# Sparse attention over paged keys and values: keys and values of a chunk loaded by different queues at different times

## The reference, cut to what matters

```
past = cache_nsa_kv[l][page_table].reshape(bs, past_len, 4, N_KV, N_HD)
...
sq = jnp.einsum('bqghd,bgqsd->bghqs', qb, kg).astype(jnp.float32) * scale + bsel
ps = masked_softmax(sq, (d >= 0)[:, :, None])
return jnp.einsum('bghqs,bgqsd->bqghd', ps.astype(vg.dtype), vg)
```

## Time and profile before

| | |
|---|---|
| median of 3 runs | 2291.73 us (2290.72 to 2292.28) |
| span of the profiled execution | 2293.0 us, its own time; no other time of it is given |
| PE busy | 2180.6 us (95%) |
| PE weight loads | 1997.7 us (87%) |
| DVE, ACT, POOL busy | 1271.6, 844.5, 592.2 us |
| mean granted TensorE clock | 0.971 of full speed |
| page chunk transfers (`na_kv<-in_pool`) | 128 from SP, 128 from POOL, 128 KB each |
| median us to landing | 3.6 (SP), 4.1 (POOL) |

### The profile page before, as it was taken

How to read it: one execution, slowest core, us unless ns; L and a number is a source line. 1 busy time by engine, 2 the same in 40 slices (tenths; PEclk the granted TensorE clock), 3 DMA queues, 4 the chain that set the end, 5 groups by cost and what they waited for, 6 DMA issues and landing times. The chain is left out here.

```text
span 2293.0 us, 42808 instructions
## 1 busy us (share of the span) xinstructions
PE 2180.6 (95%) x17107; PEld 1997.7 (87%) x17107; DVE 1271.6 (55%) x2352; ACT 844.5 (37%) x1712; POOL 592.2 (26%) x508
## 2 busy tenths in 40 slices
PE   9999998989888889999999999999899999999997
PEld 7799977865555569999999988899899999999997
DVE  2213445247666671123237145566899887876957
ACT  4221244216656560011234133553333433334443
POOL 0000025412232211211111300242344433445633
PEclk9999989979999999999999999998999999999998
DMA  4211187973453431111311156232223232265234
GB/s 152 101 44 46 37 143 236 324 279 125 131 166 111 125 128 56 60 42 56 105 63 37 38 213 244 100 131 84 89 94 117 71 122 89 85 234 186 91 119 147
DMA packets 133712, 276.33 MB, mean 121 GB/s; under 512 B 24626, under 2 KB 79571, under 8 KB 128332
## 3 DMA queue, kind: packets, MB, share of 16 engines
q1 hardware_dynamic: 110796, 232.32, 30.5%
q0 software_dynamic: 10368, 28.33, 3.8%
q10 hardware_dynamic: 12352, 12.96, 1.8%
HBM read 229.49 MB, written 48.26 MB: 121 GB/s over the span
## 5 line engine op out<-in xcount | busy, mean ns | idle before, releaser
L88 PE MATMUL psum<-merged_high,oq_half 128*128 128x352 f32 x768 | 189.0, 326 | 1.9 <-POOL oq_half L69 1.4
L88 PE MATMUL psum<-ff_t,ff_x_slots 128*128 128x264 f32 x1200 | 149.1, 284 | 1.3 <-DVE ff_x_slots L69 1.3
L88 PEld LDWEIGHTS psum<-ff_t,ff_x_slots 128*128 128x128 f32 x1200 | 147.1, 188 | 1.6 <-issue 1.5
L88 PEld LDWEIGHTS psum<-merged_high,oq_half 128*128 128x128 f32 x768 | 135.2, 190 | 2.5 <-POOL oq_half L69 1.9
L1655 POOL DMA_DIRECT2D na_kv<-in_pool x128 | 69.0, 539 | 228.0 <-PE psum L1859 157.8
L88 PE MATMUL psum<-x_half_high,mg_w_high 128*128 128x352 f32 x384 | 124.0, 323 | 2.1 <-ACT gated L2340 1.2
L88 PE MATMUL psum<-h_again_low,mg_w_high 128*128 128x352 f32 x384 | 123.1, 321 | 0.0
L88 PE MATMUL psum<-x_half_high,mg_w_low 128*128 128x352 f32 x384 | 123.0, 320 | 0.0
L1957 ACT ACTIVATE na_pt<-psum 128x512 f32<-128x512 f32 (+1 forms) x170 | 86.5, 543 | 89.3 <-PE psum L1832 80.8
L88 PE MATMUL psum<-ff_bslot,ff_x_slots 128*128 128x264 f32 x888 | 117.8, 286 | 0.7 <-DVE ff_z L4305 0.7
L88 PEld LDWEIGHTS psum<-ff_bslot,ff_x_slots 128*128 128x128 f32 x888 | 112.5, 189 | 1.0 <-DVE ff_z L4305 0.9
(11 more groups left out here) (668 smaller groups left out, 5607.0 us busy)
## 6 DMA issues: line engine op xcount, KB each, us to landing
na_kv<-in_pool SPq DMA_DIRECT2D x128, 128.0 KB, 3.6
na_kv<-in_pool POOLq DMA_DIRECT2D x128, 128.0 KB, 4.1
ff_bslot_raw<-mid_ops SPq DMA_DIRECT2D x59, 264.0 KB, 3.1
mid_ops<-ff_bufs SPq DMA_DIRECT2D x11, 1056.0 KB
mg_w<-in_w_merge SPq DMA_DIRECT2D x15, 768.0 KB, 4.5
ring<-in_f_wu SPq DMA_DIRECT2D x11, 1024.0 KB, 5.3
low<-in_f_wg SPq DMA_DIRECT2D x22, 512.0 KB, 4.5
first_pages<-in_pool SPq DMA_DIRECT2D x68, 128.0 KB, 5.7
```

What stands on the lines that cost most here:

```text
L88: ins = nc.tensor.matmul(out, w[a], x[b], start=first and n == 0, stop=last and n == 2)
```

## The change

SP loads the keys of all 16 pages of a chunk, and waits for the scores of chunk m-2 only (`scores_ready`). POOL loads the values of all 16 pages, and waits for the values of chunk m-2 (`pv_ready`), as before. Each page gives two transfers of 128 rows x 512 bytes (64 KB) in place of one of 128 KB: SP and POOL issue 16 a chunk each where they issued 8. The page numbers are read in two halves: those of sequences 0 and 1 before the slot wait, those of 2 and 3 between the eighth and the ninth transfer. PE waits for the keys at the scores and for the values at the values product. The window chunks are laid out like the page chunks and are loaded by SP as 4 transfers of keys and 4 of values, with a semaphore each. The slot wait of the chunks 0 and 1 is unchanged.

```diff
-        kv_loaded = [sem(f"kv_loaded{j}") for j in range(2)]
+        keys_loaded = [sem(f"keys_loaded{j}") for j in range(2)]
+        window_values = [sem(f"window_values{j}") for j in range(2)]
...
-        SP_PAGES, POOL_PAGES = [(b, p) for b in (0, 1) for p in range(4)], [(b, p) for b in (2, 3) for p in range(4)]
...
-        def slot_free(eng, m):
-
-            if m >= 2:
+        def slot_free(eng, m, part):
+
+            if m == 0:
+                eng.wait_ge(S["hm_kept"], 16)
+            elif m == 1:
+                eng.wait_ge(S["scores_ready"], logits_done(at[OWN_BIAS, 0, 0]))
+            elif part == KEY:
+                eng.wait_ge(S["scores_ready"], logits_done(chunk_items[m - 2]))
+            else:
                 eng.wait_ge(S["pv_ready"], order[chunk_items[m - 2]] + 1)
...
-        def load(eng, m, mine, done):
+        def load(eng, m, part, done):
             _, s, c = chunk(m)
-            page = [g for b in range(mine[0][0], mine[-1][0] + 1)
-                    for g in page_numbers(nc, eng, pages, (4 * s + b) * NPAGE + 4 * c, 4, N["n_pool"])]
-            slot_free(eng, m)
-            for (b, p), g in zip(mine, page):
-                eng.dma_start(kv[m % 2][:, b, 2 * PAGE * p:2 * PAGE * (p + 1)],
-                              A["pool"][ds(g, 1), :, 2 * PAGE:4 * PAGE].rearrange("a p x -> (a p) x")).then_inc(done[m % 2], 16)
+            for half in range(2):
+                page = [page_numbers(nc, eng, pages, (4 * s + b) * NPAGE + 4 * c, 4, N["n_pool"]) for b in (2 * half, 2 * half + 1)]
+                if half == 0:
+                    slot_free(eng, m, part)
+                for j in range(2):
+                    for p, g in enumerate(page[j]):
+                        to, x = (2 * p + part) * PAGE, (2 + part) * PAGE
+                        eng.dma_start(kv[m % 2][:, 2 * half + j, to:to + PAGE],
+                                      A["pool"][ds(g, 1), :, x:x + PAGE].rearrange("a p x -> (a p) x")).then_inc(done[m % 2], 16)
...
-                    return load(sp, m, SP_PAGES, kv_loaded)
-                slot_free(sp, m)
-                for b in range(4):
-                    sp.dma_start(kv[m % 2][:, b, :].rearrange("p (k x) -> p k x", k=2), A["winp"][4 * s + b]
-                                 ).then_inc(kv_loaded[m % 2], 16)
+                    return load(sp, m, KEY, keys_loaded)
+                slot_free(sp, m, KEY)
+                for part, done in ((KEY, keys_loaded), (VALUE, window_values)):
+                    for b in range(4):
+                        sp.dma_start(kv[m % 2][:, b, :].rearrange("p (a k x) -> p a k x", k=2, x=PAGE)[:, :, part, :],
+                                     A["winp"][4 * s + b][:, part, :].rearrange("p (a x) -> p a x", x=PAGE)).then_inc(done[m % 2], 16)
...
-                    load(pool, chunk_of[u] + 2, POOL_PAGES, kv_soft)
+                    load(pool, chunk_of[u] + 2, VALUE, kv_soft)
...
-                    pe.wait_ge(kv_loaded[m % 2], filled(m, hard))
-                    if filled(m, soft):
-                        pe.wait_ge(kv_soft[m % 2], filled(m, soft))
+                    pe.wait_ge(keys_loaded[m % 2], filled(m, hard))
...
+                if c == WINDOW:
+                    pe.wait_ge(window_values[m % 2], 64)
+                else:
+                    pe.wait_ge(kv_soft[m % 2], filled(m, soft))
```

More of the change, by code:

```diff
@@ L1633, in sparse_attention @@
         logits_done = lambda u: pieces_of[u][-1] + 1
-        SP_PAGES, POOL_PAGES = [(b, p) for b in (0, 1) for p in range(4)], [(b, p) for b in (2, 3) for p in range(4)]
         chunk = lambda m: items[chunk_items[m]]
-        hard = lambda m: 16 * (4 if chunk(m)[2] == WINDOW else len(SP_PAGES))
-        soft = lambda m: 16 * (0 if chunk(m)[2] == WINDOW else len(POOL_PAGES))
+        hard = lambda m: 16 * (4 if chunk(m)[2] == WINDOW else 16)
+        soft = lambda m: 16 * (0 if chunk(m)[2] == WINDOW else 16)
@@ L1638, in sparse_attention @@
         filled = lambda m, size: sum(size(j) for j in range(m % 2, m + 1, 2))
-        def slot_free(eng, m):
-            if m >= 2:
-                eng.wait_ge(S["pv_ready"], order[chunk_items[m - 2]] + 1)
[L1644 to L1647, removed]
-        def load(eng, m, mine, done):
-            _, s, c = chunk(m)
-            page = [g for b in range(mine[0][0], mine[-1][0] + 1)
-                    for g in page_numbers(nc, eng, pages, (4 * s + b) * NPAGE + 4 * c, 4, N["n_pool"])]
-            slot_free(eng, m)
-            for (b, p), g in zip(mine, page):
-                eng.dma_start(kv[m % 2][:, b, 2 * PAGE * p:2 * PAGE * (p + 1)],
-                              A["pool"][ds(g, 1), :, 2 * PAGE:4 * PAGE].rearrange("a p x -> (a p) x")).then_inc(done[m % 2], 16)
+        KEY, VALUE = 0, 1
@@ L1694, in _ @@
                     elif m % 2 == 0:
-                        slot_free(sp, m)
+                        slot_free(sp, m, VALUE)
                         sp.dma_start(hm, A["hm_spill"]).then_inc(S["hm_back"], 16)
@@ L1727, in page_keys @@
             def page_keys(m, b):
-                x = kv[m % 2][:, b, :]
-                return x[:, 0:CH] if chunk(m)[2] == WINDOW else x.rearrange("p (a x) -> p a x", x=2 * PAGE)[:, :, 0:PAGE]
+                return kv[m % 2][:, b, :].rearrange("p (a x) -> p a x", x=2 * PAGE)[:, :, 0:PAGE]
             def page_value(m, b, j):
-                c = CH + j * P if chunk(m)[2] == WINDOW else 2 * PAGE * j + PAGE
+                c = 2 * PAGE * j + PAGE
                 return kv[m % 2][:, b, c:c + P]
```

## The result

The changed kernel takes 2301.03 us (median of 6 runs, 2297.96 to 2304.78), the kernel before beside it 2291.07 us (6 runs). The ratio is 1.0041, with a 95% interval of 1.0025 to 1.0056: slower by 5.7 to 12.8 us, 9.4 in the middle (the two medians differ by 10.0). That is clear of the 0.2% that can be told from nothing. The profiled execution took 2301.77 us for a span of 2299.8.

What follows compares the result with a forecast made beforehand. TensorE was taken as the bound, with time won only where it stands idle. Terms -11.5 - 3.0 + 16.4 + 1.5 = +3.4 us on 2291.7 gave 2295.1 us; range 2278 to 2304, the forecast's own 2290 to 2301.

Steps and rivals of the forecast that it cites:

- rival C: At the pair ends POOL is held by a further 2.77 us pause each: 8.3 us more, 2303.4 us; chance 0.13.
- Key waits removed: TensorE's ten page-load waits at the scores, 18.6 us, all go; 7.1 us of waiting for DVE's scaling stays.
- What they were worth: Gain in the page stage: 11.5 us from load waits plus 3.0 us from two clock falls that go.
- POOL's issue is priced by rows: On POOL's queue, half the bytes in the same 128 rows costs the whole 0.536 us, 0.587 with its gap.
- Rival A: POOL's issue price goes by bytes, 0.268 + 0.051 us; strip copy 1.2 us late; -11.0, 2280.7 us; chance 0.13.
- The gap for the page numbers: Between POOL's issues 8 and 9, reading page numbers takes 0.75 us more (ends 0 and 1.1).
- The copy late by the whole addition: At three pair ends POOL's strip copy comes 5.45 us late and the delay reaches PE whole: 16.4 us lost.
- Rival B: After each pair's end PE or DVE catches up and half the delay is regained: -6, 2286 us; chance 0.07.
- The clock: Behind PE's stalls at the three pair ends, one more clock fall than now: 1.5 us lost (ends 0 and 4.5).
- The rule weighed: DVE's two-port mode locks POOL out while it writes descriptors: 4.0 us at pair ends, sum +7.4; left out.
- Rival D: Key waits stay, as SP's queue or 512-byte rows keep keys late: only losses left, +18, 2310 us; chance 0.05.
- DMA load: POOL's chunk takes 6.9 us (by bytes) to 13.8 us (by packets) of all engines, some 13 between chunks: costs nothing.

Runs made afterwards that it cites:

- strips_first: The changed kernel with the next pair's strip copies one tile earlier in GpSimd's queue, ahead of the 16 value transfers: 2277.22 us, ratio to before 0.9937.
- strips_between: The changed kernel with the strip copies between the eighth and ninth value transfer of the same load: 2278.12 us, ratio to before 0.9960.
- values_shared: The changed kernel with SyncE loading the values of two sequences behind its keys and GpSimd the other two: 2275.94 us, ratio to before 0.9950.
- keys_at_values: The changed kernel with the keys waiting for the values product of chunk m-2, as in the kernel before: 2339.59 us, ratio to before 1.0221.

## Why the prediction was right or wrong

The mechanism held and the time lies in the range, but the change is slower by more than the noise, while the forecast was 0.15%, "no change by a small margin". The 2301 us lie at the very top of the forecast's own range, 2290 to 2301; the room above it, up to 2304, was given for rival C, which is not what used it. That the time lies within is owed in part to that room. Step by step:

- **Key waits removed: held.** No page-load wait is left. The waits for L2114 (the old L2106) behind the ten page scores are 0.53 to 1.14 us, 7.9 in sum, where 0.46 to 1.09 and 7.1 were worked out. SyncE's 16 issues take 9 us and more, as above, and not 6.6; of the ten us that keys have to spare this takes some three.
- **What they were worth: too much by 2 us.** Forecast 11.5 + 3.0 us; 13.6 against the profile that it was read from, 12.3 against the mean of three. The sentence that failed is that the profiled execution stood 1.3 us above the median and "the terms don't depend on that": the waits and the two clock falls were those of one execution. Of the two, 0.8 are the longer waits for L2114.
- **POOL's issue is priced by rows: held.** 0.534 us for 512-byte rows, 0.536 for 1 KB. Rival A is out. The gap for the page numbers is 0.76 us, 0.71 more than the 0.05 between plain issues (forecast 0.75 more).
- **The copy late by the whole addition: held.** The three loads ahead of a copy took 4.97 to 4.99 us up to the copy before, each with a pause of 0.34 to 0.36 us in it, and 10.10 us after, without one. DVE's waits for it grew by 31.9 - 16.1 = 15.8 us (forecast 16.4 and "some 32 us in all"), and PE's stalls from 1.6 to 6.7 or 7.1 us. `strips_first`, `strips_between` and `values_shared` each take the loss away by the copy's place or by the number of issues ahead of it. Rival B, that half would be caught up, is out.
- **The clock: this is the term that failed most.** I counted one more fall at 1.5 us. The ends lost 21.5 us (mean), of which the late copy explains 15.8; the other 5.7 are what is left over, and I put them down to the clock. The run with 58 transposes puts the three falls of the changed kernel at 8.1 us, 2.7 each. The kernel before paid for two falls at its ends in the first two profiles and for none in the third, where the ends accordingly lost the most, 23.4 = 15.8 + 7.6. So it was not the number of falls alone: at the two ends that already had a fall it became dearer too, and the sum left those at nothing. I had priced a fall behind a load wait of 2.6 us, where 3.4 us of work met the lower level (0.57 over 4 us), and applied that to a stall of 7 us, behind which 6 us of work met it. The upper end that I gave, 4.5, was short of it too.
- **Rival C**, that POOL would be held by further pauses at the ends: none of the three loads ahead of a copy has a further pause. But the pause of 2.8 us of the earlier trace rows also stands in the load before the last at the second end, and makes POOL's queue late there (POOL's timeline):

```profile
652.07 0.53 POOL L1661 DMA_DIRECT2D na_kv<-in_pool  x1 [2.14 <-PE psum L1867]
655.39 4.10 POOL L1661 DMA_DIRECT2D na_kv<-in_pool  x7 [2.79 <-issue]
660.26 5.10 POOL L1661 DMA_DIRECT2D na_kv<-in_pool  x8 [0.77 <-issue]
665.72 4.68 POOL L1661 DMA_DIRECT2D na_kv<-in_pool  x8 [0.35 <-issue]
```

The load ahead of the copy starts at 665.72 as soon as the one before it is through, 2.14 us behind its values product, where it is 1.76 at the other two ends. That is 0.4 us, and PE's stall grew by 5.50 us there and by 5.11 and 5.12 at the others. So C was there, at 0.4 us in place of 8.3.
- **The rule weighed.** The rule of the Trainium skill (SBUF — State Buffer, "Who interferes with whom") would have added 4.0 us by my estimate. The trace of the changed kernel agrees with the rule and with leaving it out of the sum. Of its 256 issues 53 overlap in time with DVE's scaling (L2114); they took 0.599 us on average, against 0.535 for the 203 others, and 22 of the 23 issues longer than 0.56 us are among them. The longest, 1.047 us, lies in the row at 660.26 above, beside these scalings:

```profile
660.96 1.54 DVE L2114 TENSOR_SCALAR na_p<-na_p,na_rs,branch_gates 128x1024 f32<-128x1024 f32 x2
```

None of the 23 lies in the three loads ahead of a copy: where the copy is waited for, DVE is idle, which was the prediction's reason for leaving the rule out, and it held. Only at the second end may it have a share: the row at 660.26 is 0.4 us longer than the plain 4.68, and that end was 0.4 us later.
- **Rival D**, keys late in spite of the early release: none is.

Corrected: -12.3 + 15.8 + 5.7 = +9.2 us, in place of -14.5 + 16.4 + 1.5 = +3.4. The range was wide enough; its middle was 6 us low, 4.2 of it by the clock and 2.2 by the gain, less 0.6 by the copy. That weighs so much because two sums of 15 to 20 us nearly cancel.

The version that beats both kernels is the changed one with the strip copies first (0.9937, interval 0.9912 to 0.9962), one constant away; `values_shared` (0.9950) is within its interval.

## What to carry to other kernels

When a queue gets more to issue, look for what stands behind it in the same queue and not only for what waits for its transfers: here 256 landings were early enough, and three small copies behind them cost more than all the load waits that the change removed. Moving them ahead costs some 0.4 us and makes the change a gain. Price a stall of TensorE with the clock behind it, and take that price from stalls of the same length: a short one can't tell it. And where the gain is a sum of waits for transfers, read it from more than one execution.

## What the runs showed of the hardware that was not expected

- A GpSimd issue of 128 rows costs the same for 512 bytes a row as for 1 KB: 0.534 and 0.536 us.
- The engines' time per packet of SyncE's queue fell nearly with the bytes. Before, in 538 to 552 us (packets, MB, share of 16 engines' time):

```profile
q1 hardware_dynamic: 1152, 1.05, 23.8%
```

That is 46 ns a packet. After, in 641 to 655 us:

```profile
q1 hardware_dynamic: 2592, 1.18, 30.3%
```

That is 26 ns, with half the bytes. The upper end of the prediction's DMA load, price by packets, was far off.

- SyncE's issues of page transfers follow one another at 0.53 us in the kernel before and in `keys_at_values` alike, though the transfer's own instruction takes 0.333 us at the median; the rest goes to the register operations and the dispatch between.
- 22 transposes of the identity in a stall of 6.7 us left the work behind it at the lower clock; 58 held the clock at 1.00.
- GpSimd and VectorE are slower beside one another. GpSimd's issues took 0.599 us on average beside DVE's scaling and 0.535 elsewhere in the changed kernel, and two scalings of 640 columns took 1.96 to 3.09 us beside GpSimd's strip copies in `strips_first`, against 2 x 0.61 elsewhere.
